# A transformer trunk in float32 on one core: the memory's norm moved from its rows before the projections to a per-partition scale and a factor behind them

## Chip, cores, metric

One Trainium2 chip, one of its cores. The metric is the device time of one execution in microseconds (us). Three executions of the kernel before took 2705.37, 2705.79 and 2707.19 us; the median is 2705.79.

## The reference, cut to what the change touches

Two layers work on x (512 tokens by 2048 features); each ends with attention over a memory of 256 rows by 2048 features. The memory is the same in both layers and its norm depends only on `mem`:

```python
def rms_norm(x, gain):
    xf = x.astype(jnp.float32)
    y = xf * lax.rsqrt(jnp.mean(xf * xf, axis=-1, keepdims=True) + EPS)
    return (y * gain.astype(jnp.float32)).astype(x.dtype)

for layer in range(DEPTH):
    ...
    m = rms_norm(mem, mem_norm[layer])                       # mem: 256 x 2048
    y = memory_cross_attention(h, m, m_w_q[layer], m_w_kv[layer], m_w_o[layer])
# inside: k, v = jnp.split(mem_h @ w_kv, 2, axis=-1)         # w_kv: 2048 x 1024
```

Layer 0 starts with a mixer of two parts, a gated delta rule (8 heads) and a differential attention with rotary positions (8 heads); layer 1 starts with a gated convolution.

## The kernel before

**Products in three parts.** Every large product is made in float32 from a high part and a low part (rounded copy, and what the rounding left). ScalarE makes the high part, VectorE subtracts it to get the low part, and TensorE (PE) adds hi x hi, hi x lo and lo x hi into a PSUM bank (`chunk`, lines 785 to 787). Activations lie feature-major: feature on the partition, token in the free dimension, 16 tiles of 128 features in H_hi and H_lo.

**Chunks.** Weights stream through in 400 chunks of 4 k tiles by 256 columns (512 KB). Per chunk SP (the queue of SyncE) loads into one of four raw slots, ScalarE writes `w_hi` (L397), VectorE `w_lo` (L1106), and PE runs 24 products. The split of chunk g waits until chunk g-2 is used; a load waits for the low part of the chunk four before it. Four chunks make a pair of banks: `acc[0:2]` for even pairs, `acc[2:4]` for odd ones. A pair's first product waits on `acc_free` until the pair two before it has been evacuated.

**Order of the work.** Each engine has one hand-written order. Chunks 0 to 127 are the mixer's input projection, 8 iterations of 16 ("AB", `ab_round`). Iterations 1 to 4 carry in between them the steps ("hops") of the delta rule, 5 to 7 those of the attention of three head pairs. Then come 32 chunks ("KV") that project the memory to keys and values of both layers, 256 columns wide, with the attention of the fourth head pair in between; then the output projection and the rest. A hop stands at a slot (a chunk and one of its four k steps) on PE, and its replies at the same place in the orders of ScalarE and VectorE. In iterations 5 to 7: a03 and b02 in chunk 8, b03 in 9, ft0 and a10 in 10, a11 and b10 in 11, a12 and b11 in 12, a13 and b12 in 13, a14 and b13 in 14, ft1 in 15. "a" are scores (L929) and transposes of earlier probabilities (L918), "b" the product with the values (L937), "ft" the transposes of a head's output (L942), whose reply on VectorE is L1300. The reply to b03 or b13 is four row sums on ScalarE (L528), a scaling on VectorE (L1293), a power on POOL (L1676) and a product on VectorE (L1295).

**The fourth pair's rotation.** When it is done with the third pair's power, POOL makes two cosine products (L1714) for the fourth pair. In KV chunk 0 ScalarE makes four shifted copies of the queries (L506) and VectorE two products (L1273, L1275); in KV chunk 3 the same for the keys. The hops of this pair start in KV chunk 9.

**The memory, until now.** In iteration 5 SP loads `mem` row-major, one row per partition, with two DMAs of 1 MB (L320). In iteration 6 ScalarE squares it with row sums (`mem_squares`, chunks 8 and 9, two squares each), VectorE makes the mean (`mem_stat`, chunk 12), and POOL the root (L1723), between head pair 1 and the cosine products of pair 2. In iteration 7 ScalarE scales the rows (`mem_rows`, L560, chunks 8 and 9). Then, for each layer, there are eight groups of two k tiles: PE transposes four 128x128 blocks into a bank (`mem_transposes`, L954), VectorE multiplies them by the gain from PSUM into one of two buffers (L1373), ScalarE makes the high part (`mem_high`, L567), VectorE the low part (`mem_low`, L1367). Group g waits for the gain product of group g-2, whose bank it takes. The groups of layer 0 stand in the k steps of chunks 14 and 15 of iteration 7, those of layer 1 in KV chunks 1 and 2. Group 0 of layer 1 also waits until the last AB pair is evacuated, which VectorE does in KV chunk 0 (L1327, behind the split of KV chunk 1).

**Keys and values.** `take_kv` copies a pair's two banks: to the keys directly, for values to `v_feat`, from which PE makes transposes (`value_transposes`, L989), which are copied to `mv`.

The lines that set the waits:

```python
pe.wait_ge(*MV(f"m{l}{g - 2}"))        # mem_transposes, g >= 2
pe.wait_ge(acc_free, 2 * (P_KV - 1 + l))   # mem_transposes, g == 0
act.wait_ge(*MV(f"m{l}{g}"))           # mem_high
```

## Time and profile before

| what | before |
|---|---|
| median of three executions | 2705.79 us |
| profiled execution, first to last instruction (span) | 2700.1 us |
| instructions | 30903 |
| PE busy | 2516.7 us, 93% |
| VectorE (DVE) busy | 1286.9 us, 48% |
| ScalarE (ACT) busy | 827.3 us, 31% |
| GpSimd (POOL) busy | 306.6 us, 11% |
| mean granted clock of PE | 0.972 |
| moved between HBM and the chip | 84 GB/s over the span |

The profile is of one execution. Its own total isn't recorded, only its span, which is 5.7 us under the median. Busy time counts instructions at work on data; PE's products are pipelined, so that one that is listed with 0.39 us may start 0.23 us after the one before. A granted clock of 1.00 is 2.4 GHz, 0.50 is 1.2 GHz. "<-" and a releaser behind an idle time name what the engine waited for.

### The profile page before, as it was taken

To read this page: it belongs to the slowest core of one execution; us is meant where nothing else is said; L and a number is where in the kernel's file an instruction comes from. 1 tells how busy PE (TensorE), PEld (TensorE's weight loads), DVE (VectorE), ACT (ScalarE), POOL (GpSimd) and SP (SyncE) were. 2 spreads that over 40 slices of the span, in tenths; PEclk is the share of its full clock that TensorE was granted. 3 is DMA by queue.
4 is the path that set the end of the run, shared out by engine and by line. 5 is a ranking of instruction groups with operands and counts; after the bars stand their busy time and mean duration, and the time that the engine had idled before them with its cause. 6 is when DMAs were issued, how large, how long until landed. Compare 5 with 4: busy or idle time off the path is not lost.

```text
span 2700.1 us, 30903 instructions
## 1 busy us (share of the span) xinstructions
PE 2516.7 (93%) x12300; PEld 2082.1 (77%) x12300; DVE 1286.9 (48%) x1667; ACT 827.3 (31%) x1344; POOL 306.6 (11%) x204
## 2 busy tenths in 40 slices
PE   7999999999999998989979979999999999998896
PEld 6787787878877777878857758888888888887665
DVE  4654555454455557552355465433433344324645
ACT  4232323232344344442242441222212222223332
POOL 3020110102100100001140140000000000012204
PEclk9999999999999999999989979999999999998898
DMA  9522322175344331452212213333332333232112
GB/s 168 86 61 48 63 47 63 47 62 55 72 113 83 78 86 63 139 170 98 94 55 70 78 47 94 94 97 97 93 96 90 101 98 96 94 101 71 62 63 78
DMA packets 221153, 227.78 MB, mean 84 GB/s; under 512 B 9328, under 2 KB 214384, under 8 KB 220784
## 3 DMA queue, kind: packets, MB, share of 16 engines
q1 hardware_dynamic: 220896, 225.64, 33.4%
q8 instruction: 84, 1.38, 0.2%
q10 hardware_dynamic: 144, 0.52, 0.1%
q14 instruction: 29, 0.24, 0.0%
HBM read 221.94 MB, written 4.19 MB: 84 GB/s over the span
## 4 chain that ended last, share of the span: by engine, by line
PE 57%; issue 25%; DVE 7%; POOL 6%; ACT 4%; DMA 1%; DVEq 0%; SPq 0%; POOLq 0%; ACTq 0%
PE acc L785 18%; PE acc L786 17%; PE acc L787 17%; POOL residual L1744 3%; POOL work L1699 2%; DVE weights_lo L1106 2%; ACT work L506 1%; ACT weights_hi L397 1%; DVE work L1514 1%; ACT work L707 1%; PE m L1023 1%; POOL small L1676 1%; PE m L929 1%; PE m L1049 1%; PE m L1061 1%
## 5 line engine op out<-in xcount | busy, mean ns | idle before, releaser
L785 PE MATMUL acc<-input_hi,weights_hi 128*128 128x512 f32 (+1 forms) x3200 | 1266.4, 396 | 82.6 <-DVE input_lo L1508 42.9
L787 PE MATMUL acc<-input_hi,weights_lo 128*128 128x512 f32 (+1 forms) x3200 | 1234.0, 386 | 2.4 <-issue 2.4
L786 PE MATMUL acc<-input_lo,weights_hi 128*128 128x512 f32 (+1 forms) x3200 | 1234.7, 386 | 0.0
L1106 DVE TENSOR_TENSOR weights_lo<-weights_raw,weights_hi 128x1024 fp32r<-128x1024 f32 x400 | 502.5, 1256 | 918.3 <-ACT weights_hi L397 918.0
L785 PEld LDWEIGHTS acc<-input_hi,weights_hi 128*128 128x128 f32 x3200 | 612.4, 191 | 227.0 <-issue 66.4
L397 ACT ACTIVATE weights_hi<-weights_raw 128x1024 fp32r<-128x1024 f32 x400 | 423.2, 1058 | 993.1 <-PE acc L787 980.0
L787 PEld LDWEIGHTS acc<-input_hi,weights_lo 128*128 128x128 f32 x3200 | 611.9, 191 | 121.4
L786 PEld LDWEIGHTS acc<-input_lo,weights_hi 128*128 128x128 f32 x3200 | 612.7, 191 | 111.8 <-issue 1.9
L1736 POOL TENSOR_TENSOR work<-work 128x512 f32<-128x512 f32 x56 | 72.3, 1291 | 1145.8 <-ACT work L661 1141.8
L1676 POOL TENSOR_TENSOR small<-small 128x4 f32<-128x4 f32 (+1 forms) x20 | 25.5, 1273 | 789.7 <-DVE small L1293 417.0
L1744 POOL TENSOR_TENSOR residual<-residual,work 128x512 f32<-128x512 f32 x58 | 91.8, 1613 | 43.7 <-DVE work L1514 43.7
L1699 POOL TENSOR_TENSOR work<-work,constants 128x1024 f32<-128x1024 f32 x24 | 61.2, 2551 | 175.2 <-PE m L861 94.3
L867 PE MATMUL m<-work 128*128 128x128 f32 x320 | 60.2, 287 | 8.3 <-ACT work L473 8.3
L1313 DVE SCALAR_TENSOR_TENSOR work<-work,parameters 128x511 f32<-128x511 f32 (+2 forms) x72 | 59.6, 827 | 8.7 <-DVE work L1310 1.7
L661 ACT ACTIVATE work<-work 128x512 f32<-128x512 f32 x64 | 39.3, 632 | 69.2 <-DVE work L1486 69.2
L867 PEld LDWEIGHTS m<-work 128*128 128x128 f32 x320 | 48.8, 202 | 9.7 <-ACT work L473 9.7
L681 ACT ACTIVATE input_hi<-residual,parameters 128x512 fp32r<-128x512 f32 x48 | 34.7, 723 | 68.8 <-POOL residual L1744 68.8
L545 ACT ACTIVATE work<-work 128x512 f32<-128x512 f32 x24 | 15.1, 631 | 132.0 <-DVE work L1313 128.5
L1226 DVE TENSOR_TENSOR work<-work,m 128x1024 f32<-128x1024 f32 x16 | 19.5, 1222 | 73.4 <-PE m L867 73.2
L1514 DVE SCALAR_TENSOR_TENSOR work<-work,parameters,m 128x512 f32<-128x512 f32 x64 | 45.9, 737 | 12.4 <-PE m L764 12.4
L473 ACT ACTIVATE work<-m 128x1024 f32<-128x1024 f32 x20 | 20.5, 1024 | 99.3 <-PE m L861 99.3
L1508 DVE SCALAR_TENSOR_TENSOR input_lo<-residual,parameters,input_hi 128x512 fp32r<-128x512 f32 x48 | 48.7, 1020 | 2.5 <-ACT input_hi L681 2.5
(225 smaller groups left out, 1788.5 us busy)
## 6 DMA issues: line engine op xcount, KB each, us to landing
weights_raw<-in_ab_w_in SPq DMA_DIRECT2D x128, 512.0 KB, 5.2
weights_raw<-in_c_w_in SPq DMA_DIRECT2D x128, 512.0 KB, 3.6
weights_raw<-in_m_w_kv SPq DMA_DIRECT2D x32, 512.0 KB, 3.4
weights_raw<-in_ab_w_out SPq DMA_DIRECT2D x32, 512.0 KB, 3.3
weights_raw<-in_m_w_q SPq DMA_DIRECT2D x32, 512.0 KB, 3.4
weights_raw<-in_c_w_out SPq DMA_DIRECT2D x32, 512.0 KB, 3.3
residual<-in_x SPq DMA_DIRECT2D x32, 256.0 KB, 5.2
weights_raw<-in_m_w_o SPq DMA_DIRECT2D x16, 512.0 KB, 3.2
```

Of the source, the lines that this page charges most:

```text
L397: act.activation(w_hi[:, s * CW:(s + 1) * CW], raw[:, c * CW:(c + 1) * CW], ACT.Copy)\
L785: pe.matmul(out, w_hi[:, o:o + P], hi(kt), start=kt == 0, stop=False)
L786: pe.matmul(out, w_hi[:, o:o + P], lo(kt), start=False, stop=False)
L787: last = pe.matmul(out, w_lo[:, o:o + P], hi(kt), start=False, stop=kt == last_kt)
L867: last = pe.matmul(m(m01, h, t), prod[:, o(h, t)], inv_t[:, o(h, t)], start=True, stop=True)
L1106: TTO(w_lo[:, s * CW:(s + 1) * CW], raw[:, c * CW:(c + 1) * CW], w_hi[:, s * CW:(s + 1) * CW].bitcast(F32), ALU.subtract).then_inc(lo_read ...
L1313: STT(out=dst[:, d:T], in0=conv_in[:, 0:T - d], scalar=tap(3 - d), in1=dst[:, d:T], op0=ALU.mult, op1=ALU.add).then_inc(*EV.did(f"c{sec}{n ...
L1514: STT(out=yt(k), in0=yt(k), scalar=pcol(post, layer * KT + k), in1=M[1], op0=ALU.mult, op1=ALU.mult)\
L1676: return pool.tensor_tensor(dst[:, 0:n], src[:, 0:n], minus_half[:, 0:n], ALU.pow)
L1699: pool.tensor_tensor(tiles(c_t), tiles(n_t), over_tiles(level_mask(s), 8), ALU.mult)\
L1736: pool.tensor_tensor(acc_sq, acc_sq, sqt[:, (k % 2) * T:(k % 2 + 1) * T], ALU.add)\
L1744: pool.tensor_tensor(xt(k), xt(k), yt(k), ALU.add).then_inc(*(NG if r < 3 else FG).did(f"x{k}"))
```

## The change

`mem` comes from the host transposed, as 16 tiles of 128 features by 256 rows, and is loaded with four DMAs of 512 KB, the form of the weights' loads. The gain is now a scale per partition: ScalarE's high part is a copy with scale (two of 128x256 per group), VectorE's low part a multiply and subtract in one instruction (two per group). Both read the loaded memory itself; the transposes, the gain product, the row scaling and the two buffers go. The groups of layer 0 stay in chunks 14 and 15 of iteration 7, those of layer 1 go to KV chunks 1 to 8, one in each, behind the split and ahead of the evacuations and hops.

The row's root is applied later: `take_kv` multiplies the banks by it. For it, squares are summed over the 16 tiles: in iteration 6 ScalarE squares four tiles in each of chunks 8 to 11, VectorE sums four tiles each in chunks 9 to 12 (a reduction with a stride of 256 elements, and an add from the second on), each square waits for the sum before it. PE sums over the partitions ahead of KV chunk 1, waiting for the last AB pair's evacuation; VectorE makes the mean, POOL the power (now between the fourth pair's cosine products and its first power), PE spreads it into rows ahead of KV chunk 3, VectorE copies them into `rs`, and PE waits for this ahead of KV chunk 4.

The diff, with its context cut ("..." where lines are left out):

```diff
--- before.py
+++ after.py
@@ -235,11 +235,11 @@
         v_feat = wk(2 * MEM)
+        mem_sum, mem_part = v_feat[:, 0:MEM], v_feat[:, MEM:2 * MEM]
         kv_at = work_w - 4 * MH * MEM
...
         mk, mv = wk(2 * MH * MEM, kv_at), wk(2 * MH * MEM)
-        mem_tok = work[:, kv_at:kv_at + 2 * D]
-        mem_scaled = (tanh_t[:, 0:T], tanh_t[:, T:2 * T])
+        mem_in_sb = work[:, kv_at:kv_at + KT * MEM]
@@ -259,14 +259,14 @@
         yt = lambda k: Y[:, bass.ds(k * T, T)]
-        mem_g = lambda H, l, g: H[:, (l * 8 + g) * T:(l * 8 + g + 1) * T]
+        mem_k = lambda k: mem_in_sb[:, k * MEM:(k + 1) * MEM]
         mem_h = lambda H, l, k: H[:, l * KT * MEM + k * MEM:l * KT * MEM + (k + 1) * MEM]
...
             sem(n) for n in ("params_in", "consts_in", "tables_in", "gate_in", "reloaded", "out_done"))
-        x_in, mem_in = [sem(f"x_in{k}") for k in range(KT)], [sem(f"mem_in{m}") for m in range(2)]
+        x_in, mem_in = [sem(f"x_in{k}") for k in range(KT)], [sem(f"mem_in{g}") for g in range(4)]
         raw_in = [sem(f"raw_in{n}") for n in range(RAW_SLOTS)]
@@ -316,9 +316,9 @@
                         sp.wait_ge(*GA("end", 3))
-                        for m in range(2):
-                            sp.dma_start(mem_tok[:, m * D:(m + 1) * D], dram["mem"][m * P:(m + 1) * P, :])\
-                                .then_inc(mem_in[m], 16)
+                        for g in range(4):
+                            sp.dma_start(mem_in_sb[:, 4 * g * MEM:4 * (g + 1) * MEM].rearrange("p (k n) -> p k n", k=4),
+                                         dram["mem"][4 * g:4 * g + 4].rearrange("k p n -> p k n")).then_inc(mem_in[g], 16)
                     load_pair(dram["ab_w_in"], col + sec, C_AB + 16 * like + 4 * j, n)
@@ -545,26 +545,20 @@
-            def mem_squares(m):
-                act.wait_ge(mem_in[m], 16)
-                for h in range(2):
-                    if h or m:
-                        act.wait_ge(*MA.last())
-                    act.activation(tanh_t, mem_tok[:, m * D + h * 2 * T:m * D + (h + 1) * 2 * T], ACT.Square,
-                                   accum_out=t1[:, 2 * h + m:2 * h + m + 1]).then_inc(*MA.did("ss"))
-            def mem_rows(m):
-                act.wait_ge(*MG("pow"))
-                o = slice(m * D, (m + 1) * D)
-                act.activation(mem_tok[:, o], mem_tok[:, o], ACT.Copy, scale=t2[:, m:m + 1]).then_inc(*MA.did(f"n{m}"))
+            def mem_squares(g):
+                act.wait_ge(mem_in[g], 16)
+                if g:
+                    act.wait_ge(*MV(f"sum{g - 1}"))
+                act.activation(tanh_t, mem_in_sb[:, 4 * g * MEM:4 * (g + 1) * MEM], ACT.Square)\
+                    .then_inc(*MA.did(f"sq{g}"))
...
                     act.wait_ge(chunk_used, C_KV - 2 if l == 0 else C_KV)
-                act.wait_ge(*MV(f"m{l}{g}"))
-                act.activation(mem_g(H_hi, l, g), mem_scaled[g % 2][:, :], ACT.Copy).then_inc(*MA.did(f"hi{l}{g}"))
+                for k in (2 * g, 2 * g + 1):
+                    act.activation(mem_h(H_hi, l, k), mem_k(k), ACT.Copy, scale=pcol("mem_norm", l * KT + k))\
+                        .then_inc(*MA.did(f"hi{l}{k}"))
@@ -592,12 +586,10 @@
                     split(C_AB + 16 * like + c + 1, it - like)
-                    if like == 6 and c in (8, 9):
+                    if like == 6 and 8 <= c < 12:
                         if c == 8:
...
                         mem_squares(c - 8)
-                    if like == 7 and c in (8, 9):
-                        mem_rows(c - 8)
                     if like == 0:
@@ -642,9 +634,8 @@
                 split(C_KV + c + 1)
-                for k in range(4):
-                    if 1 <= c <= 2:
-                        mem_high(1, 4 * (c - 1) + k)
+                if 1 <= c <= 8:
+                    mem_high(1, c - 1)
                 if c in (0, 3):
@@ -942,19 +933,6 @@
-            def mem_transposes(l, g):
-                if g == 0:
-                    pe.wait_ge(*MA("n1"))
-                    pe.wait_ge(acc_free, 2 * (P_KV - 1 + l))
-                if g >= 2:
-                    pe.wait_ge(*MV(f"m{l}{g - 2}"))
-                for n in range(4):
-                    k, m = 2 * g + n // 2, n % 2
-                    last = pe.transpose(acc[2 * l + g % 2][:, n * P:(n + 1) * P],
-                                        mem_tok[:, m * D + k * P:m * D + (k + 1) * P], ident)
-                last.then_inc(*MM.did(f"t{l}{g}"))
             def ab_round(it, like):
@@ -964,8 +942,6 @@
                                 hop(name, i)
-                        if like == 7 and c >= 14:
-                            mem_transposes(0, 4 * (c - 14) + k)
                     if like == 0 and c == 8:
@@ -989,21 +965,32 @@
+            def mem_rms(c):
+                if c == 1:
+                    pe.wait_ge(*MV("sum3"))
+                    pe.wait_ge(acc_free, 2 * P_KV)
+                    for m in range(2):
+                        last = pe.matmul(acc[2][:, m:m + 1], mem_sum[:, m * P:(m + 1) * P], ones, start=True, stop=True)
+                    last.then_inc(*MM.did("ss"))
+                elif c == 3:
+                    pe.wait_ge(*MG("pow"))
+                    rows(lambda m: acc[3][:, m * P:(m + 1) * P], lambda m: t2[:, m:m + 1], 2).then_inc(*MM.did("rows"))
+                elif c == 4:
+                    pe.wait_ge(*MV("rms"))
             for c in range(32):
...
                 def between(k):
-                    if 1 <= c <= 2:
-                        mem_transposes(1, 4 * (c - 1) + k)
                     if k % 2:
...
                     value_transposes(q // 4, q % 4, P_KV + q)
-                if c % 16 == 0 or c == 4:
-                    pe.wait_ge(*MV(f"m{int(c > 0)}7"))
+                mem_rms(c)
                 chunk(C_KV + c, P_KV + c // 4, 4 * (c % 4), KT - 1, width=MEM, between=between,
-                      ready=(lambda kt: MV(f"lo{l}{kt // 2}")) if c % 16 < 4 else None,
+                      ready=(lambda kt: MV(f"lo{l}{kt}")) if c % 16 < 4 else None,
                       hi=lambda k: mem_h(H_hi, l, k), lo=lambda k: mem_h(H_lo, l, k))
@@ -1353,29 +1340,31 @@
-            def mem_stat():
-                dve.wait_ge(*MA("ss"))
-                TTO(t1[:, 4:6], t1[:, 0:2], t1[:, 2:4], ALU.add).then_inc(*MV.did())
-                dve.wait_ge(*MV.last())
-                TS(t1[:, 6:8], t1[:, 4:6], 1.0 / D, EPS, ALU.mult, ALU.add).then_inc(*MV.did("stat"))
+            def mem_add(g):
+                dve.wait_ge(*MA(f"sq{g}"))
+                dve.reduce_sum(mem_part if g else mem_sum, tanh_t.rearrange("p (k t) -> p t k", k=4), axis=AX.X)\
+                    .then_inc(*MV.did(f"sum{g}" if g == 0 else None))
+                if g:
+                    dve.wait_ge(*MV.last())
+                    TTO(mem_sum, mem_sum, mem_part, ALU.add).then_inc(*MV.did(f"sum{g}"))
...
-                def low(g):
-                    dve.wait_ge(*MA(f"hi{l}{g}"))
-                    TTO(mem_g(H_lo, l, g), mem_scaled[g % 2][:, :], mem_g(H_hi, l, g).bitcast(F32), ALU.subtract)\
-                        .then_inc(*MV.did(f"lo{l}{g}"))
-                dve.wait_ge(*MM(f"t{l}{g}"))
-                dve.wait_ge(*MV.last())
-                gain = p_("mem_norm")[:, l * KT + 2 * g:l * KT + 2 * g + 2]
-                rows_of = lambda t: t.rearrange("p (k n) -> p k n", n=MEM)
-                TTO(rows_of(mem_scaled[g % 2][:, :]), rows_of(acc[2 * l + g % 2][:, :]), over_row(gain, 2, MEM), ALU.mult)\
-                    .then_inc(*MV.did(f"m{l}{g}"))
-                if g:
-                    low(g - 1)
-                if g == 7:
-                    low(g)
+                for k in (2 * g, 2 * g + 1):
+                    dve.wait_ge(*MA(f"hi{l}{k}"))
+                    STT(out=mem_h(H_lo, l, k), in0=mem_k(k), scalar=pcol("mem_norm", l * KT + k),
+                        in1=mem_h(H_hi, l, k).bitcast(F32), op0=ALU.mult, op1=ALU.subtract).then_inc(*MV.did(f"lo{l}{k}"))
+            def mem_rms(c):
+                if c == 1:
+                    dve.wait_ge(*MM("ss"))
+                    TS(t1[:, 0:2], acc[2][:, 0:2], 1.0 / D, EPS, ALU.mult, ALU.add).then_inc(*MV.did("stat"))
+                elif c == 3:
+                    dve.wait_ge(*MM("rows"))
+                    dve.tensor_copy(rs[:, 0:MEM], acc[3][:, 0:MEM]).then_inc(*MV.did("rms"))
+                    dve.wait_ge(*MV.last())
@@ -1409,8 +1398,8 @@
                     split(C_AB + 16 * like + c + 1, it - like)
-                    if like == 6 and c == 12:
-                        mem_stat()
+                    if like == 6 and 9 <= c < 13:
+                        mem_add(c - 9)
                     if like == 0:
@@ -1438,9 +1427,9 @@
                         if j < 2:
-                            dve.tensor_copy(mkt(l, 2 * j + n), bank(pair, n, MEM)).then_inc(acc_free, 1)
+                            TTO(mkt(l, 2 * j + n), bank(pair, n, MEM), rs[:, 0:MEM], ALU.mult).then_inc(acc_free, 1)
                         else:
-                            dve.tensor_copy(v_feat[:, n * MEM:(n + 1) * MEM], bank(pair, n, MEM))\
+                            TTO(v_feat[:, n * MEM:(n + 1) * MEM], bank(pair, n, MEM), rs[:, 0:MEM], ALU.mult)\
                                 .then_inc(*MV.did(f"vf{l}{j}"))
@@ -1464,9 +1453,9 @@
                         keep(7, 2, n)
-                if 1 <= c <= 2:
-                    for k in range(4):
-                        mem_low(1, 4 * (c - 1) + k)
+                if 1 <= c <= 8:
+                    mem_low(1, c - 1)
+                mem_rms(c)
                 if c in (0, 3):
@@ -1712,15 +1701,15 @@
                     pool.tensor_tensor(head2(dst), head2(src), cos, ALU.mult).then_inc(*BG.did("cos_" + tag))
+                if i == 3:
+                    pool.wait_ge(*MV("stat"))
+                    pool.tensor_tensor(t2[:, 0:2], t1[:, 0:2], minus_half[:, 0:2], ALU.pow).then_inc(*MG.did("pow"))
                 for h in range(2):
...
                 attention_pair(i)
-                if i == 1:
-                    pool.wait_ge(*MV("stat"))
-                    pool.tensor_tensor(t2[:, 0:2], t1[:, 6:8], minus_half[:, 0:2], ALU.pow).then_inc(*MG.did("pow"))
@@ -1788,7 +1777,7 @@
                                  np.asarray(b_out_norm).T, everywhere(a_A_log), everywhere(a_dt_bias)], axis=1)
-    arrays = {"x": np.ascontiguousarray(np.asarray(x)[0].T).reshape(KT, P, T), "mem": np.asarray(mem)[0], "constants": shape_constants(),
+    arrays = {"x": np.ascontiguousarray(np.asarray(x)[0].T).reshape(KT, P, T), "mem": np.ascontiguousarray(np.asarray(mem)[0].T).reshape(KT, P, MEM), "constants": shape_constants(),
               "parameters": np.ascontiguousarray(parameters), "lambda": np.ascontiguousarray(everywhere(b_lambda)),
```

## Rows read from the trace of the kernel before

**Rows 1.** The page, busy time of PE: us, share of span, instructions.

```profile
PE 2516.7 (93%) x12300; PEld 2082.1 (77%) x12300; DVE 1286.9 (48%) x1667; ACT 827.3 (31%) x1344; POOL 306.6 (11%) x204
```

**Rows 2.** Stretches, all engines: length, busy (count) per engine, granted clock, DMA share, GB/s.

```profile
900.00:910.00 10.00, 10.00 (x48) 7.71 (x48) 4.48 (x15) 3.76 (x11) 0.00 (x0) 1.00 0.43 94
930.00:940.00 10.00, 9.29 (x46) 7.55 (x45) 6.95 (x5) 3.15 (x10) 7.37 (x4) 1.00 0.27 59
1040.00:1050.00 10.00, 6.37 (x28) 4.77 (x27) 9.50 (x10) 3.48 (x5) 4.70 (x2) 0.83 0.17 54
```

**Rows 3.** Stretches, PE alone: length, busy (count), granted clock, DMA share, GB/s.

```profile
1028.70:1096.10 67.40, 53.84 (x349) 0.90 0.24 79
1042.90:1046.40 3.50, 0.12 (x1) 0.93 0.00 0
1046.40:1049.10 2.70, 2.66 (x9) 0.50 0.61 200
...
1083.40:1087.00 3.60, 3.60 (x20) 0.53 0.73 236
1087.00:1097.00 10.00, 10.00 (x85) 1.00 0.43 129
```

**Rows 4.** Waits of PE from 1028.7 to 1096.1 us: total, times, longest.

```profile
PE acc L954 <- DVE work L1373: 8.0, 4, 3.6
...
PE acc L785 <- DVE weights_lo L1106: 2.1, 1, 2.1
```

**Rows 5.** Groups by shape, whole span: count, busy us, mean ns, idle before.

```profile
L1532 DVE TENSOR_REDUCE work<-work 128x128 f32<-128x2048 f32 x12 | 45.5, 3808 | 0.0
L1581 DVE TENSOR_REDUCE small<-m 128x4 f32<-128x1024 f32 x8 | 9.8, 1224 | 5.7 <-PE m L1049 5.7
L1282 DVE TENSOR_REDUCE small<-m 128x2 f32<-128x1024 f32 x8 | 9.8, 1223 | 0.3
...
L1288 DVE SCALAR_TENSOR_TENSOR work<-work,small 128x256 f32<-128x256 f32 x8 | 3.9, 485 | 0.3
L1441 DVE COPY work<-acc 128x256 f32<-128x256 f32 x8 | 3.0, 416 | 0.0
...
L397 ACT ACTIVATE weights_hi<-weights_raw 128x1024 fp32r<-128x1024 f32 x400 | 423.2, 1058 | 993.1 <-PE acc L787 980.0 <-DMA weights_raw<-in_ab_w_in 11.6 <-issue 0.6
```

**Rows 6.** Instructions in time from 1039 us: POOL, VectorE, ScalarE (start, us, instruction).

```profile
1039.56 5.14 POOL L1714 TENSOR_TENSOR work<-work 128x1024 f32<-128x1024 f32 x2
...
1040.23 0.68 DVE L1373 TENSOR_TENSOR work<-acc,parameters 128x512 f32<-128x512 f32 x1
1040.83 1.66 DVE L1367 TENSOR_TENSOR input_lo<-work,input_hi 128x512 fp32r<-128x512 f32 x1
1042.56 3.23 DVE L1106 TENSOR_TENSOR weights_lo<-weights_raw,weights_hi 128x1024 fp32r<-128x1024 f32 x1
...
1053.27 4.30 ACT L506 ACTIVATE work<-work 32x1024 f32<-32x1024 f32 x4
```

**Rows 7.** Instructions in time, iteration 6, chunks 9 and 10: VectorE, ScalarE, PE.

```profile
890.84 1.22 DVE L1106 TENSOR_TENSOR weights_lo<-weights_raw,weights_hi 128x1024 fp32r<-128x1024 f32 x1 [1.72 <-ACT weights_hi L397]
...
898.84 0.75 DVE L1300 SCALAR_TENSOR_TENSOR residual<-m,small,residual 128x512 f32<-128x512 f32 x1 [0.78 <-PE m L942]
...
892.93 0.27 ACT L528 ACTIVATE work<-m 128x128 f32<-128x128 f32 x1
...
900.12 0.49 PE L929 MATMUL m<-work 64*128 64x128 f32 x4
```

**Rows 8.** PE's instructions in time, AB chunk 14, around the first transposes.

```profile
1030.18 0.60 PE L954 MATMUL acc<-constants,work 128*128 128x128 f32 x4
1030.54 0.48 PE L785 MATMUL acc<-input_hi,weights_hi 128*128 128x512 f32 x1
1030.85 0.40 PE L786 MATMUL acc<-input_lo,weights_hi 128*128 128x512 f32 x1
1031.09 0.39 PE L787 MATMUL acc<-input_hi,weights_lo 128*128 128x512 f32 x1
```

## The prediction

> **What bounds the kernel now.** I read the page first: TensorE (PE) is busy for 93% of the span [rows 1], so a change pays only where PE stands still, runs at half clock, or does work that can go. Next the stretches around the edited code: from 900 to 910 us, where the memory's squares are taken, PE is full; the statistic's power lies in the stretch from 930, with 0.71 us idle; from 1040 PE is only 6.37 us busy in 10 [rows 2]. From the start of AB chunk 14 of the last iteration to the end of KV chunk 8 there pass 67.4 us, of which PE is busy 53.8: 13.6 us idle. Inside, a stretch of 3.5 us with PE idle is followed by 2.7 us at a granted clock of 0.50, which is 1.2 GHz, and another stretch of 3.6 us at 0.53 begins at 1083; then, with 85 products in 10 us, it is back at 2.4 GHz [rows 3]. The waits name the holder: 8.0 us of PE's idle time there are its memory transposes (L954) waiting for VectorE's gain product (L1373), 2.1 us in one piece are the weight split [rows 4], and that piece is the one ahead of 1083. The chain per group of four transposes is PE, VectorE product, ScalarE high part, VectorE low part, and all of it sits inside PE's instruction order. So the edited code is itself on the path.
>
> The sum is made against the profiled execution: its span is 2700.1 us, the median of the runs 2705.8, so 5.7 us lie around the span or between runs; its own total is not shown. I carry differences over to the median unchanged. A measurement of this kernel can tell about 0.2% (5.4 us) from no change.
>
> **Part by part.**
> Loads. Two DMAs of 1 MB become four of 512 KB in runs of 1 KB, the form of the weight loads. They are issued an iteration and a half before their first reader, with PE full in between; SP gains two issues. Nothing, unless the transfer took some 100 us.
>
> Squares and sums (AB iteration 6). ScalarE's four squares stay four, one per chunk. New on VectorE are four reductions 128x256<-128x1024 over elements 1 KB apart, and three adds. The trace has no such reduction at this size. From PSUM, contiguous, 1024 elements take 1223 ns; over 2 KB strides from SBUF 2048 take 3808 ns, which halved is 1.9 us [rows 5]. If the surplus of that row (about 1.6 us over contiguous) belonged to its 128 outputs, 12.5 ns each, 256 outputs would make 1.2+3.2=4.4 us; but 4 outputs cost what 2 cost (1224 against 1223) [rows 5]. I take 1.9, as that row is nearest, and keep 1.2 and 4.4. The Trainium skill's page "SBUF — State Buffer" (section "Door 1: The DMA port swizzle", its box on cachelines) says that an access that crosses into another 16-byte line pays a penalty. By that rule the surplus is per element, so its sum is that with 1.9, and it speaks against the change. These reductions stand ahead of the attention replies on VectorE, and the next square waits for the last sum. Worked through with rows 7: VectorE's split ends at 892.0, first sum 893.9, second square 894.9, so the four row sums of hop b03 start 2.0 us later than 892.9; the norm and the rotation hop stay in time. In chunk 10 the split is then over at 899.1, reduction and add at 901.5, L1300 (0.75) at 902.2 instead of 899.6. PE's scores L929 at 900.1 need it: PE stops 2.2 us. In chunks 11 and 12 the same delays end within PE's margin by my working. Cost 2.2 us, plus 0.9 us for a half-clock stretch (a whole one of 3.4 us loses half of it, 1.7; I take half of that, as the stop is short and PE was full before). With reductions of 1.2 us the stop is 0.8; with 4.4 it is 7 us at chunk 10 and another 1 to 2 behind.
>
> Power. It leaves POOL's queue ahead of the cosine products of pair 2, behind which VectorE's split and then PE are late; PE is 9.29 us busy in the 10 [rows 2]. I take all of that 0.7 as gained. In its new place, POOL is free.
>
> Row scaling on ScalarE (two of 2 us, iteration 7). PE is full there: nothing.
>
> Transposes and gain products. 64 transposes go. Each of the 16 groups of four holds PE 0.36 us, and the product behind it takes 0.31 to the next start instead of 0.24 [rows 8]: 0.43 a group, 7 us at full clock. VectorE loses, per group of two k tiles, a product of 0.68 [rows 6] and a subtraction of like size, with ScalarE between them; it gains two three-operand instructions of 128x256. L1288 of that size takes 485 ns [rows 5], some 0.40 from start to start where one follows the other: 0.8 us. ScalarE has two scaled copies; its split copy takes 1058 ns at four times the width [rows 5], so with a fixed part about 0.45 each, 0.9 a pair.
>
> The new order from 1028.7 on, by these prices. PE: two wide chunks of 24 products at 0.23 us [rows 8], with hops of 1.8 us, done at 1041.8. ScalarE reaches the row sums of b13 at 1036.0 (1.2 earlier, three transpose groups), so POOL's two cosine products start at 1038.4 instead of 1039.6 [rows 6]. Now the price of a shared resource. In rows 6 VectorE's L1373, with one operand in PSUM, takes 0.68 while POOL is at work; L1367 and L1106, whose two tensors lie in SBUF, take 1.66 and 3.23 (L1106 alone 1.22 [rows 7]). The edit turns the former kind into the latter. The Trainium skill, same page, section "Who interferes with whom", calls this an exclusive lock for the whole instruction on DVE instructions with two SBUF inputs. The trace agrees: L1106 ends 1.09 us after POOL's pair does, nearly its whole time alone. The low parts of k tiles 6 and 7 thus end at 1043.9 and the split of KV chunk 0 at 1045.1 (if the new instruction passed POOL as L1373 does, 3 us earlier, and 3 us more gain). PE idles 3.3 us, then runs chunk 0, partly at half clock (1.4 more), to 1049.4. VectorE: four low groups 3.2, L1300 0.7, split of chunk 1 1.2, two evacuations 1.3: 1051.3. PE needs these last for its new sum of squares, whose bank they free: 1.9 us idle. Chunks 1, 2 and 3 then run nearly back to back (2.88 us each, 85 products in 10 us [rows 3]; 1.5 more for the clock); the three new waits of the statistic (scaling, power, row copy, some 2 us together) fit within chunk 2 and the splits, the last at 1062.4. Then ScalarE's four rotation copies (4.30 [rows 6]) start behind the high part, at 1060.7, end at 1065.0, and VectorE goes on with two rope instructions of 1.2 and the split of chunk 5: 1068.7. PE idles 3.4 us, again with 1.7 us of clock. Chunk 8 ends at 1082.0 against 1096.1: **gain 14.1 us**. What is left is 8.6 us of idle time; late next is the rope chain.
>
> Later low parts (chunks 4 to 8): splits 1.05 on ScalarE [rows 5] and 1.22 on VectorE per 2.88 us, plus 0.9 and 0.8: covered. Without that cover each chunk would lose up to 0.8. Evacuations with the root: 0.416 for a copy [rows 5], at most the 0.485 of the three-operand form: 0.07 each; eight of the 16 stand ahead of value transposes: below 0.6, taken as nothing. From chunk 9 on both kernels run the same order, shifted; SP's loads follow the splits, so they shift too.
>
> **Sum**: 14.1 + 0.7 - 2.2 - 0.9 = 11.7 us. Span 2688.4, median **2694.1**.
>
> **Rivals.**
> 1. More of it goes: the stops don't lower the clock (5.5 us were taken off for it), the reduction takes 1.2 (1.4 more), or VectorE's new instructions meet POOL less (3.0); about half of these 9.9 us gives 2689. For: PE has no transposes between its products any more. Against: the stop of 2.1 us ahead of 1083 was followed by half clock too [rows 3, 4]. Chance 0.17.
> 2. Only PE's work leaves: rope, splits and the new waits fill the freed time, which gives the 7 us of the transposes alone: 2698.8. For: the rope chain is untouched, and PE waits at three new places (sum bank, power, rows). Against: of the old idle time 8.0 us was the transposes' own wait. Chance 0.13.
> 3. The reductions are priced by output, 4.4 us each: 8 to 9 us of stops and some 2 of clock in iteration 6: gain 14.1+0.7-10.5=4.3, 2701.5. Against: the equal rows for 2 and 4 outputs. Chance 0.09.
> 4. Slower: the same reductions, square waiting for sum and attention reply waiting behind both, cost more than the transposes. From 1.9 to 4.4 us each the loss grows by about 3 us per us; it overtakes the gain of 14.8 at 6 us a reduction, and at 8 would give 2712 (gain 14.8 less 21.3). The row of twice the elements takes 3.8, so only a row of 1 KB strides that behaves quite otherwise does it. Chance 0.03.
> 5. The change doesn't do what it says: the chain isn't shorter, as the high and low parts still wait for something old. The diff takes the transposes out of both queues, so this comes down to rival 2.
>
> **Numbers.** Forecast 0.58, rivals 0.17, 0.13, 0.09, 0.03. Faster: forecast, 1 and 2, 0.88; same: 3, 0.09; slower 0.03. The range goes from 2688 (rival 1) to 2701 (up to rival 3).
>
> **What would show it.** Right: PE's product count 12300-64+4=12240; no wait of PE on a VectorE product; KV chunk 0 starts some 6.5 us earlier counted from AB chunk 14; two or three idle stretches of 2 to 3.5 us left, before chunks 0, 1 and 5; the reductions near 1.9 us and one stop of 2 us at L929 in iteration 6. Wrong: reductions over 3 us, stops in chunks 11 to 13 of iteration 6, or PE waiting at the row products for the power.

## The result, and the profile after

The changed kernel takes 2690.15 us (median) against 2706.49 us of the kernel before in the same comparison: ratio 0.9938, 95% interval 0.9925 to 0.9952. One of its four executions was slow (12514 us at a mean granted clock of 0.188); it counts in this median, not in the ratio, and the median of the other three is 2688.01. A second set of executions gave 2693.27 us and 0.9946 (0.9925 to 0.9967). So the kernel is faster by 0.5 to 0.6%; 2694.1 was forecast.

The page after, the lines that answer to [rows 1] and to the table before:

```profile
span 2690.5 us, 30792 instructions
...
PE 2513.4 (93%) x12244; PEld 2078.9 (77%) x12244; DVE 1286.4 (48%) x1674; ACT 826.7 (31%) x1354; POOL 306.4 (11%) x204
```

The span fell by 9.6 us, where 11.7 were forecast (2688.4). Line numbers are those of the changed kernel from here on: products L776 to L778 (were L785 to L787), weight split L1093 (L1106), scores L920 (L929), reply to ft L1287 (L1300), product of the b13 reply L1282 (L1295), last AB evacuation L1314 (L1327), POOL's powers L1665 (L1676), cosine products L1703 (L1714).

Stretches of PE alone, as in [rows 3] (length, busy, granted clock, DMA share, GB/s); the first again runs from the start of AB chunk 14 to the end of KV chunk 8:

```profile
1034.10:1086.30 52.20, 44.91 (x293) 0.90 0.32 101
1047.20:1050.10 2.90, 0.01 (x1) 0.85 0.00 0
1050.30:1056.20 5.90, 5.31 (x24) 0.51 0.29 90
1069.70:1073.00 3.30, 0.00 (x0) 1.00 0.00 0
1073.00:1076.50 3.50, 3.49 (x16) 0.52 0.47 151
```

67.4 us became 52.2. Two stops of over 1 us are left, of 2.9 us ahead of KV chunk 0 and 3.3 ahead of chunk 5, each with a granted clock of half behind it. KV chunk 0 starts 7.0 us earlier, counted from AB chunk 14 (16.0 us behind it instead of 23.0). PE's waits in the same stretch, as in [rows 4]: no transpose waits for a gain product any more; the split is what is late.

```profile
PE acc L776 <- DVE weights_lo L1093: 6.3, 2, 3.3
PE acc L974 <- DVE work L1314: 0.8, 1, 0.8
PE acc L776 <- DVE rstd_rows L1366: 0.3, 1, 0.3
```

The new instructions by shape, whole span (count, busy us, mean ns): reduction, low part, evacuations, high part, square and what it waited for.

```profile
L1346 DVE TENSOR_REDUCE work<-work 128x256 f32<-128x1024 f32 x4 | 7.9, 1971 | 0.0
...
L1356 DVE SCALAR_TENSOR_TENSOR input_lo<-work,parameters,input_hi 128x256 fp32r<-128x256 f32 x32 | 17.3, 591 | 0.0
L1430 DVE TENSOR_TENSOR work<-acc,rstd_rows 128x256 f32<-128x256 f32 x8 | 3.0, 415 | 0.0
...
L560 ACT ACTIVATE input_hi<-work,parameters 128x256 fp32r<-128x256 f32 x32 | 14.0, 500 | 0.0
L552 ACT ACTIVATE work<-work 128x1024 f32<-128x1024 f32 x4 | 4.2, 1054 | 11.6 <-DVE work L1350 8.3 <-DVE work L1346 3.2
```

The loss in iteration 6, as VectorE's instructions in time; then the same stretch for all engines, which was full in [rows 2]:

```profile
900.35 1.22 DVE L1093 TENSOR_TENSOR weights_lo<-weights_raw,weights_hi 128x1024 fp32r<-128x1024 f32 x1
901.48 1.93 DVE L1346 TENSOR_REDUCE work<-work 128x256 f32<-128x1024 f32 x1
903.45 0.42 DVE L1350 TENSOR_TENSOR work<-work 128x256 f32<-128x256 f32 x1
903.79 0.74 DVE L1287 SCALAR_TENSOR_TENSOR residual<-m,small,residual 128x512 f32<-128x512 f32 x1
```

```profile
900.00:910.00 10.00, 7.95 (x32) 5.91 (x31) 7.70 (x14) 2.92 (x6) 0.00 (x0) 0.83 0.30 52
940.00:950.00 10.00, 9.94 (x46) 8.03 (x46) 6.93 (x5) 2.12 (x2) 4.96 (x2) 1.00 0.44 104
```

L1287 stands behind reduction and add, and PE's scores stop 2.05 us for it, with a mean clock of 0.83 in these 10 us. POOL's power has left its old place, and the stop of 0.71 us [rows 2] is gone; no experiment parts this from the rest of the edit.

**Where the time went, by marks.** POOL's eight small powers of the attention (4 wide) are marks that both kernels have. From one to the next, in us, the last column being the sum from the second to the eighth:

| | 2-3 | 3-4 | 4-5 | 5-6 | 6-7 | 7-8 | sum |
|---|---|---|---|---|---|---|---|
| before | 66.63 | 37.83 | 67.31 | 39.09 | 98.11 | 44.65 | 353.62 |
| changed | 68.74 | 39.55 | 66.66 | 37.85 | 84.11 | 44.64 | 341.55 |

Iteration 6's sums cost 2.11+1.72 = 3.83 us (2-3, 3-4); POOL's power gave 0.65 (4-5); three transpose groups ahead of hop b13 gave 1.24 (5-6); the keys and values 14.00 (6-7). Together 12.07 us. (The span fell by less because the second power stands at 829.96 us instead of 827.72; in the second profiles of both kernels, experiments 1 and 2, it stands at 828.03 and 826.97.) Inside 6-7 the stops on PE of over 0.25 us went from 14.01 to 7.93 us, and the time lost to a clock under full (each half microsecond times what its granted clock is short of 1) from 6.82 to 5.12. It comes in steps of 1.71 us, at half of full clock (1.2 of 2.4 GHz). So of the 14.0 us some 6.1 are shorter stops, 1.7 clock, and 5.6 (an estimate: 13 groups of transposes at the forecast's 0.43) PE's own work; the sum is rough, as some of the half clock lies within stops.

### The profile page after: what moved, and what is told of

It is laid out like the page before. It is cut to its first block, busy times and chain, and to the rows that moved or that the text cites. A ratio compares the mean times of both kernels' runs of the same rounds, so it can differ in the third digit from the quotient of the medians.

```text
span 2690.5 us, 30792 instructions
## 1 busy us (share of the span) xinstructions
PE 2513.4 (93%) x12244; PEld 2078.9 (77%) x12244; DVE 1286.4 (48%) x1674; ACT 826.7 (31%) x1354; POOL 306.4 (11%) x204
## 4 chain that ended last, share of the span: by engine, by line
PE 57%; issue 25%; DVE 7%; POOL 6%; ACT 4%; DMA 1%; DVEq 0%; SPq 0%; POOLq 0%; ACTq 0%
PE acc L776 18%; PE acc L778 17%; PE acc L777 17%; POOL residual L1733 3%; POOL work L1688 2%; DVE weights_lo L1093 2%; ACT work L506 1%; ACT weights_hi L397 1%; DVE work L1503 1%; PE m L1010 1%; ACT work L698 1%; POOL small L1665 1%; PE m L1036 1%; DMA weights_raw<-in_ab_w_in 1%; PE m L1048 1%
## 5 line engine op out<-in xcount | busy, mean ns | idle before, releaser
L776 PE MATMUL acc<-input_hi,weights_hi 128*128 128x512 f32 (+1 forms) x3200 | 1267.9, 396 | 84.3 <-DVE input_lo L1497 43.5
L778 PE MATMUL acc<-input_hi,weights_lo 128*128 128x512 f32 (+1 forms) x3200 | 1236.4, 386 | 0.0
L1093 DVE TENSOR_TENSOR weights_lo<-weights_raw,weights_hi 128x1024 fp32r<-128x1024 f32 x400 | 498.4, 1246 | 916.7 <-ACT weights_hi L397 916.2
L776 PEld LDWEIGHTS acc<-input_hi,weights_hi 128*128 128x128 f32 x3200 | 613.9, 192 | 226.8 <-issue 61.2
L778 PEld LDWEIGHTS acc<-input_hi,weights_lo 128*128 128x128 f32 x3200 | 612.5, 191 | 121.4
L1665 POOL TENSOR_TENSOR small<-small 128x4 f32<-128x4 f32 (+1 forms) x20 | 25.5, 1273 | 766.8 <-DVE small L1280 392.7
L1300 DVE SCALAR_TENSOR_TENSOR work<-work,parameters 128x511 f32<-128x511 f32 (+2 forms) x72 | 59.6, 828 | 8.7 <-DVE work L1297 1.7
```

Of the source, the lines that this page charges most:

```text
L776: pe.matmul(out, w_hi[:, o:o + P], hi(kt), start=kt == 0, stop=False)
L778: last = pe.matmul(out, w_lo[:, o:o + P], hi(kt), start=False, stop=kt == last_kt)
L1093: TTO(w_lo[:, s * CW:(s + 1) * CW], raw[:, c * CW:(c + 1) * CW], w_hi[:, s * CW:(s + 1) * CW].bitcast(F32), ALU.subtract).then_inc(lo_read ...
L1300: STT(out=dst[:, d:T], in0=conv_in[:, 0:T - d], scalar=tap(3 - d), in1=dst[:, d:T], op0=ALU.mult, op1=ALU.add).then_inc(*EV.did(f"c{sec}{n ...
L1665: return pool.tensor_tensor(dst[:, 0:n], src[:, 0:n], minus_half[:, 0:n], ALU.pow)
```

## Experiments

In the profiles below the marks of untouched stretches agree within 0.1 us or differ by steps of about 1.7 us, while medians of one kernel move by 2 to 3 us from one set of executions to the next. So each verdict rests on the marks, and ratios stand beside them. "A" is the theory that each expectation names first. Each kernel but that before and the changed one has one profile, so a difference of one or two of the clock's steps between two kernels isn't by itself an effect of the edit. In the cuts of code "..." stands for lines left out.

**1. The changed kernel again.**

> The changed kernel again, unaltered. The one execution profiled so far has a span of 2690.5 us against 2700.1 of the kernel before, 9.6 us less, while the medians stand 16 us apart. Theory A: the edited code is worth 12 us (15.2 in the stretch around the keys and values, 0.7 for POOL's power, less 3.8 in iteration 6) and the rest is a difference between executions of one kernel, outside the edit: ratio to the kernel before 0.993 to 0.996, and the marks of iterations 1 to 4 stand differently from execution to execution. Rival B: something outside the stretches that I read was also made shorter by the edit, by some 4 us every time; then a new profile shows it in the same place again.

2693.27 us, ratio 0.9946 (0.9925 to 0.9967), span 2691.3. Marks: 68.73, 39.49, 66.68, 37.85, 85.25, 44.68, sum 342.68. The same stretches, except that the keys and values took 1.1 us more. Chunk 0 lost one step of clock instead of two, so that the stop ahead of chunk 1 was 1.99 us instead of 0.77; the other step came to those around chunk 5, where no later stop swallows it. Chunk 0 on PE, which in the first profile had a clock of 0.51:

```profile
1048.10:1052.40 4.30, 4.26 (x24) 0.69 0.38 122
```

No other stretch had become shorter: A, with the ratio in its range.

**2. The kernel before again.**

> The kernel before, unaltered, for a second profile of it. Its first profile has a span of 2700.1 us, 5.7 below the median, while other kernels lie 1.8 above their spans. Theory A: that execution was a quick one, by work outside the edit (the loop iterations before iteration 5, the part after the keys and values); a second one has the marks of iteration 6 to the last power of POOL at 353.6 us again within 1.7 (half a stretch at half clock), and a span of 2700 to 2706. Rival: the marks themselves are longer than in the first profile, so the edit is worth more than the 12 us that I read.

Ratio 0.9997 (0.9984 to 1.0011), span 2703.8. Marks: 66.71, 37.85, 67.31, 39.09, 100.24, 44.66, sum 355.86. From the last power's successor (the first sum of squares of the output projection) to the end it took 1482.4 us against 1480.2. So A in part: 2.2 us of the difference lie outside the edit; but the marks moved by 2.24, more than the 1.7 that I allowed, with one more step of clock (8.54 lost) and longer stops (15.8 us in all for 14.0); this is what the rival said. With two profiles of each the edit is worth 10.9 to 14.3 us by the marks.

**3. What the sums cost.** Three of the four sums of squares are left out:

```diff
-                dve.reduce_sum(mem_part if g else mem_sum, ...)
-                if g: ... TTO(mem_sum, mem_sum, mem_part, ALU.add)
+                if g == 0: dve.reduce_sum(mem_sum, ...)
+                else: dve.memset(mem_part[:, 0:1], 0.0)
...
```

> Leaves out three of the four sums of squares (only the first four k tiles enter the memory's root). Theory A: the stop of 2.05 us at the scores L920 in chunk 10 of iteration 6 and the half clock behind it are due to the second reduction and its add on VectorE, so both go: 3.5 to 3.8 us less than the changed kernel. Rival: the stop comes from the square on ScalarE that stands between the attention replies; it is still there and still waits for VectorE in its order, so at least half of the stop stays and the gain is under 2 us.

2688.20 us, ratio 0.9931 (0.9911 to 0.9952). 2-3 stays at 68.75 (the first reduction still delays b03 by two), 3-4 falls from 39.5 to 35.85, and PE has no stop in chunk 10: 3.6 us. A.

**4. The sums in another form** (nothing left out): squares of two tiles at a time in alternating halves, contiguous adds.

```diff
-                act.activation(tanh_t, mem_in_sb[:, 4 * g * MEM:4 * (g + 1) * MEM], ACT.Square)
+                act.activation(tanh_t[:, (g % 2) * T:(g % 2 + 1) * T] if g else v_feat, mem_in_sb[:, g * T:(g + 1) * T], ACT.Square)
...
-                dve.reduce_sum(mem_part if g else mem_sum, tanh_t.rearrange("p (k t) -> p t k", k=4), axis=AX.X)
+                TTO(v_feat, v_feat, tanh_t[:, (g % 2) * T:(g % 2 + 1) * T], ALU.add)
...
```

(PE's sum over the partitions now has four products instead of two.)

> The sum of squares kept whole, but made of two tiles at a time: ScalarE squares 128x512 in each of chunks 8 to 15 into alternating halves of its buffer, VectorE adds them contiguously into a 512-wide sum (seven adds of about 0.7 us), and PE sums both halves. Theory A: what costs in iteration 6 is the 2.4 us that VectorE needs ahead of each attention reply, with ScalarE in lock step; at 0.7 us and with double buffering the stop at L920 is gone, and the stretch from one power of POOL to the next that holds chunk 10 goes from 39.5 to about 36 us, like that of the run with one sum, though nothing is left out: 3.5 us less than the changed kernel. Rival: any VectorE work ahead of the replies delays them, and it is now in seven chunks instead of four: a stop of 1 us or more in chunk 10 or later.

2688.88 us, ratio 0.9930 (0.9915 to 0.9944). 2-3 is 66.68 and 3-4 37.83, the values of the kernel before: 3.7 us less than the changed kernel, no stop. The stretch forecast at 36 is 37.83, as the two stretches share the gain: the two marks around b03 move too. 6-7 came out at 86.97 here, where but for PE's two more products the code is the changed kernel's: a stop of 3.12 us ahead of chunk 1, and two steps of clock that begin in this stop and last through chunk 1, where no later stop swallows them (table below experiment 7). The sum of the marks is therefore 340.68, only 0.9 and 2.0 less than in the two profiles of the changed kernel.

**5. POOL ahead of VectorE.** The cosine products of the fourth pair before the third pair's last power, on their own semaphore:

```diff
+                    if i == 2 and h == 1:
...
+                        pool.wait_ge(*BM("a14", 2))
+                        for src, dst, tag in ((qc, qr, "q"), (kc, kr, "k")):
+                            pool.tensor_tensor(head2(dst), head2(src), cos, ALU.mult).then_inc(*EG.did("cos_" + tag))
                     pool.wait_ge(*BV(f"stat{h}", i))
...
```

> POOL makes the fourth pair's two cosine products ahead of the third pair's last power instead of behind it, as soon as hop a14 is done, on a counter of its own. Theory A: PE's stop of 2.91 us ahead of KV chunk 0 is VectorE held off by POOL in instructions with two tensors in SBUF; the 5 us of POOL then lie under a wait of VectorE for hop b13, the split of chunk 0 comes some 4 us earlier, PE's stop there goes, and all behind it moves: 3 to 4.5 us less than the changed kernel. Rival: VectorE is simply full there (6.8 of 10 us busy, with queue behind the row sums); then chunk 0 starts under 1 us earlier. Second rival: chunk 0 starts early, but chunk 1 waits the same time more, as it hangs on VectorE's queue and not on PE: under 1.5 us less.

2692.75 us, ratio 0.9952 (0.9933 to 0.9971). VectorE's low parts in the changed kernel's second profile, and in this one:

```profile
1036.00 2.46 DVE L1356 SCALAR_TENSOR_TENSOR input_lo<-work,parameters,input_hi 128x256 fp32r<-128x256 f32 x6
...
1042.43 4.52 DVE L1356 SCALAR_TENSOR_TENSOR input_lo<-work,parameters,input_hi 128x256 fp32r<-128x256 f32 x2
```

```profile
1034.88 6.76 DVE L1357 SCALAR_TENSOR_TENSOR input_lo<-work,parameters,input_hi 128x256 fp32r<-128x256 f32 x6
...
1043.45 0.87 DVE L1357 SCALAR_TENSOR_TENSOR input_lo<-work,parameters,input_hi 128x256 fp32r<-128x256 f32 x2
```

Wherever POOL's 5 us lie, the low parts that meet them stand still: two take 4.52 instead of 0.87, or six take 6.76 instead of 2.46. That shows the contention of [rows 6] on the new instruction. But moved ahead it delays the row-sum reply by 2.15 us (5-6 is 40.00), the stop ahead of chunk 0 falls from 2.90 to 1.27, and the one ahead of chunk 1 grows to 3.12. From power 5 to 7: 121.88 against 121.96 and 123.10 of the changed kernel. A's size fell, and the gain is that of the second rival, under 1.5 us. But its mechanism isn't what the trace shows: counted from power 5, chunk 1 starts 1.5 us earlier (49.95 instead of 51.47), just as chunk 0 does (43.70 instead of 45.22); the stop ahead of it is longer because chunk 0 ran at full clock. The gain is lost behind that, as chunk 1 now has the half clock:

```profile
1051.80:1055.90 4.10, 4.10 (x23) 0.62 0.37 124
```

**6. The transposes put back as load.** 32 transposes of a constant in chunks 14 and 15:

```diff
+                        if like == 7 and c >= 14:
...
+                            for n in range(4):
+                                pe.transpose(acc[k % 2][:, n * P:(n + 1) * P], ident, ident)
```

> Puts the 32 transposes of layer 0 back into PE's order in chunks 14 and 15 (of a constant; nobody reads them, and they wait for nothing but free banks). Theory A: they hold PE 0.43 us per group of four, 3.4 us in all, but only the three groups ahead of hop b13 delay the chain of row sums, power, cosine products and split that ends PE's stop before KV chunk 0; the other five fall into that stop of 2.9 us: 1.3 us (1 to 2) more than the changed kernel. Rival: PE's own work counts in full: 3.4 us more.

2693.82 us, ratio 0.9962 (0.9946 to 0.9978). 5-6 is 39.12 (1.27 more), 6-7 is 85.38; from power 5 to 7 124.50 against 121.96 and 123.10. The stop ahead of chunk 0 fell from 2.9 to 0.67 us: five groups went into it, and chunk 0 starts 1.3 us later. A, for three groups count at once and five are swallowed. This load waits for no gain product: that the waits themselves cost what [rows 4] says is read from the traces before and after, and no experiment put them back.

**7. Layer 1's groups back in KV chunks 1 and 2.**

```diff
-                if 1 <= c <= 8:
-                    mem_low(1, c - 1)
+                if 1 <= c <= 2:
+                    for k in range(4):
+                        mem_low(1, 4 * (c - 1) + k)
```

(and the same for `mem_high`)

> The changed kernel with the eight groups of layer 1 back in KV chunks 1 and 2, four in each, where the kernel before had them. It parts what the spreading over chunks 1 to 8 brings from what the removal of the transposes brings. Theory A: VectorE is the late engine from the end of AB chunk 15 to KV chunk 2, so 3.2 us more of low parts ahead of the statistic and of the next split in each of chunks 1 and 2 come nearly in full: PE stops ahead of chunks 2 and 3, 4 to 6 us more than the changed kernel. Rival: the low parts fit into VectorE's waits for ScalarE's rotation copies: under 1.5 us more.

2693.39 us, ratio 0.9951 (0.9937 to 0.9966). 6-7 is 86.92, 1.7 and 2.8 us more than in the two profiles of the changed kernel, which is above the rival's 1.5. But experiment 4, which has the changed kernel's placement and the same stop of 3.12 ahead of chunk 1, has 86.97. The only stop that grew is that for the row copy, 0.28 to 0.92, and the one ahead of chunk 5 shrank from 3.33 to 3.16. Set beside experiment 4 my theory fell and the rival holds: VectorE still waits 2.67 us for ScalarE's rotation copies of the keys, so the low parts ahead of them delay nothing behind. Spreading them over eight chunks brought nothing that these runs show; the medians (2693.39, and 2693.27 in experiment 1) agree.

The starts in us, counted from power 5, show where the profiles part:

| | chunk 0 | sum ahead of chunk 1 | chunk 5 | power 7 |
|---|---|---|---|---|
| changed | 45.22 | 51.47 | 68.10 | 121.96 |
| changed again | 45.21 | 51.46 | 68.09 | 123.10 |
| 4, sums by pairs | 45.21 | 51.47 | 70.99 | 124.82 |
| 5, POOL ahead | 43.70 | 49.95 | 67.93 | 121.88 |
| 6, transposes as load | 46.52 | 52.77 | 70.74 | 124.50 |
| 7, groups in two chunks | 45.19 | 51.44 | 70.94 | 124.75 |

From chunk 0 to the sum there are 6.25 us in every row: VectorE's queue sets that start, and half clock on chunk 0 is swallowed in front of it. Half clock on chunk 1 is not, and makes the 2.9 us by which experiments 4 and 7 start chunk 5 later than the changed kernel.

**8. The keys' rotation spread.**

```diff
-                if c in (0, 3):
-                    attn("begin_k" if c else "begin", 3)
+                if c == 0:
+                    attn("begin", 3)
+                if 3 <= c <= 6:
...
+                    rot_part(kc, "rk", c - 3)
```

(ScalarE; VectorE's `begin_k` in chunk 6)

> ScalarE makes the four shifted copies of the keys one in each of KV chunks 3 to 6 instead of all in chunk 3, and VectorE its two products in chunk 6. Theory A: PE's stop of 3.3 us ahead of KV chunk 5 is this block of 4.3 us on ScalarE with VectorE and its split behind it, and half clock follows the stop: both go, less some 0.5 us because ScalarE then has 3.0 us of work per chunk of 2.88: 4 to 5 us less than the changed kernel in the stretch around the keys and values. Rival: VectorE is the engine that is late there (splits, low parts, evacuations), so the stop moves to chunks 6 and 7: under 2 us less.

2687.75 us, ratio 0.9929 (0.9918 to 0.9941). 6-7 is 81.80 against 84.11 and 85.25. The stop of 3.3 ahead of chunk 5 is gone and one of 1.12 comes later, ahead of chunk 8; the clock loses 3.42 us, one step less than in both profiles of the changed kernel. 2.3 to 3.5 us less, where A said 4 to 5 and the rival under 2: A's mechanism, but a third of the stop moved on, as in the rival.

**9. Both rotations spread, with the sums by pairs.**

> The sums by pairs of tiles, and both rotations of the fourth head pair spread: queries copied in KV chunks 1 to 4, keys in 5 to 8, with VectorE's products in chunks 4 and 8. Theory A: stops ahead of KV chunks 0 (2.9 us, POOL) and 1 (2.0, the bank of the last AB pair) stay, the one ahead of chunk 5 and all of iteration 6 go: 7 to 9 us less than the changed kernel, so 18 to 21 less than the kernel before by the marks in the trace, and a ratio near 0.992 or below. Rival: two spreads load ScalarE for eight chunks with more than a chunk's time, and the stops come back from chunk 5 on: no better than the sums by pairs alone.

2687.91 us, ratio 0.9933 (0.9920 to 0.9946), sum of the marks 338.02, 15.6 less than the kernel before in its first profile, not 18 to 21, and 3.5 to 4.7 less than the changed kernel, not 7 to 9. 6-7 is 84.34: behind chunk 4 come stops of 1.13, 0.92, 0.29 and 0.36 us. It is 2.7 us less than the sums by pairs alone, so the rival falls as it was put; but it is 2.1 more than with the keys alone spread (experiment 10), and the stops came back as it said: ScalarE with split, two high parts and a copy has 1.06+0.89+1.06 us, more than a chunk of 2.88, for eight chunks.

**10. The two parts that paid, together** (4 and 8).

> Sums by pairs of tiles, and the keys' shifted copies spread over KV chunks 3 to 6. Theory A: both gains add, as they lie in different stretches: 3.7 us in iteration 6 and 1.7 to 3.4 in the stretch around the keys and values (81.8 to 83.5 us from power to power against 84.1 to 85.3): 5.5 to 7 us less than the changed kernel, ratio to the kernel before near 0.992. Rival: as with both rotations spread, part of the second gain comes back as half clock: under 4.5 us less.

2687.43 us, ratio 0.9926 (0.9913 to 0.9940), 6-7 82.20, sum 335.93: 5.6 and 6.8 us less than the two profiles of the changed kernel. A.

**11. Four parts**: 4, 8, 5, and the partition sum one chunk later (`if c == 2` for `if c == 1` in both `mem_rms`).

> As the kernel with sums by pairs and spread key copies, and also the early cosine products on POOL and the partition sum of squares one chunk later (ahead of KV chunk 2), so that chunk 1 doesn't wait for the last AB pair's evacuation. Theory A: VectorE is the late engine from the end of AB chunk 15 to chunk 2. The early products give it 1.2 to 1.5 us; the later sum lets PE start chunk 1 some 1.3 us earlier but doesn't move chunk 2, which hangs on VectorE's next split: another 1 to 2 us less than the kernel with two parts, and the stop ahead of chunk 1 falls from 3.1 to under 2 while one of about 1 us appears ahead of chunk 2 or 3. Rival: PE's wait for the bank was the limit, and all of its 3.1 us come off: 3 us or more less.

2684.11 us, ratio 0.9909 (0.9895 to 0.9923), 5-6 39.99, 6-7 77.52, sum 333.34. PE's waits from AB chunk 14 on:

```profile
PE acc L784 <- DVE weights_lo L1103: 4.3, 3, 1.8
```

2.6 us less than with two parts by the marks, and 1.7 of it is one step of clock, so that 0.9 is left for the edit. The wait for the bank is gone, one of 1.8 for the split takes its place. That is A for the wait; the stop of about 1 us ahead of chunk 2 or 3 didn't come (0.35 us ahead of the row products of chunk 3), and the size, forecast at 1 to 2, is 0.9 or 2.6, depending on whether the step is counted. It is the fastest kernel of this study, with an interval below that of the changed kernel.

## Why the prediction was right, step by step

- **Main stretch.** 14.1 us forecast, 15.2 measured (67.4 to 52.2). The stops came as worked out: ahead of KV chunk 0 3.3 forecast, 2.9 measured; ahead of chunk 1 1.9, measured 0.8 and 2.0; ahead of chunk 5 3.4, measured 3.3. The clock loss of 4.6 was 5.1. Which product it falls on decides whether a later stop swallows it; that alone moved 6-7 by 1.1 us in the same code. (The prediction adds VectorE's 3.2, 0.7, 1.2 and 1.3 us from 1045.1 to 1051.3; they make 1051.5.)
- **PE's share of the transposes.** 0.43 us a group: three groups gave 1.24, and put back they cost 1.27. Shown. That the rest is the waits for VectorE's gain product rests on the traces alone: 8.0 us of them before [rows 4], none after.
- **The shared resource.** The forecast had low parts 6 and 7 end 5.5 us after the start of POOL's cosine products (1038.4 to 1043.9); they ended 5.2 us after it (1043.74 to 1048.94). Experiment 5 shows that the hold follows POOL. Its price, given as "3 us earlier, and 3 us more gain", is not shown: experiment 5 moved the meeting and didn't remove it, so chunks 0 and 1 started 1.5 us earlier, and at power 7 0.1 to 1.2 us was left.
- **The strided reduction.** 1.9 forecast, 1.97 measured, against 1.2 and 4.4 at the ends; the stop at L920 2.2 forecast, 2.05 measured. The surplus goes with the element, not with the output: 1.92 ns an element at 1 KB strides with 256 outputs, 1.86 in L1521 at 2 KB with 128. The Trainium skill's "SBUF — State Buffer" says in the section on Door 1 that each access that crosses to a new 16-byte line pays a penalty, and the trace agrees. The term that I had too small is the clock behind the stop: 0.9 forecast, 1.7 measured in five of the six profiles with this stop; in the sixth (experiment 5, 3-4 at 37.99) PE stopped as long and the clock stayed full.
- **POOL's power**: 0.7 forecast, 0.65 measured.
- **Evacuations and high parts.** 0.415 against 0.416 for the copy: nothing, as taken. The high part took 0.50 alone, 0.42 from start to start.
- **Product count.** "12300-64+4=12240" is 12244: I counted two products for the sum of squares and two for the rows, and the trace lists each of them twice, as the rows by shape show; 12300-64+4+4=12244.

```profile
L755 PE MATMUL acc<-constants,small 128*128 128x128 f32 x4 | 0.6, 273 | 0.0
L974 PE MATMUL acc<-constants,work 128*128 128x1 f32 x4 | 0.6, 248 | 0.8 <-DVE work L1314 0.8
```

- **The sum against the median.** 12.07 us by the marks and 11.7 forecast agree, in part by luck: the main stretch gave 1.1 us more than forecast and iteration 6 cost 0.7 more, and the two offset each other. The medians stand 16.3 us apart in the first comparison and 10.7 in the second; the means of 50 executions before and 7 of the changed kernel stand 14.6 apart. The marks gave 10.9 to 14.3 in two profiles of each. The span of the first profile before was quick: a second one was 3.7 us longer. Carrying a difference over from one profiled execution has that error in it, and I gave no allowance for it. That this is why the first result lies near the quick end of the range isn't shown; the second set, 2693.27, lies at the forecast.

Of the rivals, the first (more goes, 2689) is nearer to the measured 2690.15 than the forecast is, though none of its three reasons came true: half clock followed the stops, the reduction took 1.97 us, and the low parts were held off beside POOL. The second is contradicted by the stops (PE idle 7.3 us instead of 13.6 in the main stretch), the third and fourth by the 1.97 us.

## What to carry to other kernels

A layout that saves TensorE transposes pays three times where they stand in its order: their own time, the waits for their evacuation, and the half clock behind the longer of these waits (here behind stops of 1.8 to 3.6 us, though not behind each). Price the new work on the helper engines in the place where it stands in their queue: four reductions of 2 us ahead of an attention reply took a quarter of the gain, and as contiguous adds with two buffers they took nothing. And before spreading work over more chunks, look whether the engine waits there anyway.

## What the runs showed of the hardware that I had not expected

The loss to the clock comes in equal parts: 1.70 to 1.71 us per stretch at half clock, in every profile, 6.82 us for four of them in the kernel before and 8.54 for five in its second profile. The same code may have one more or one less, and they fall on other products each time. So a single profile compares two kernels only to about 2 us here, however well its untouched stretches agree (37.84, 37.83, 37.82 us between the first two powers).
